# First pair's operand remainders on VectorE, and the down projection's first buffers placed slot by slot and loaded from a new point

## The reference, cut to what matters

```python
def _conv_ffn(h, conv_prev, w_up, conv_w, conv_b, w_down):
    u = h @ w_up                                   # 1024 -> 2 * 2816
    L = u.shape[1]
    ext = jnp.concatenate([conv_prev.astype(u.dtype), u], axis=1)
    c = conv_b + sum(conv_w[j] * ext[:, j:j + L] for j in range(FFN_CONV))
    gate, val = jnp.split(c, 2, axis=-1)
    return (jax.nn.silu(gate) * val) @ w_down, ext[:, -(FFN_CONV - 1):]
```

## Time and profile before

| what | value |
|---|---|
| median of 3 runs | 3153.21 us (3151.97 to 3154.39) |
| profiled execution, its own time | 3155.45 us |
| its span, first to last instruction | 3153.7 us |
| TensorE busy (matmuls) | 3041.2 us, 96% |
| VectorE busy | 1603.9 us, 51% |
| ScalarE busy | 1232.1 us, 39% |
| GpSimd busy | 1069.9 us, 34% |
| mean granted TensorE clock | 0.990 |

### The profile page before, as it was taken

The page is one execution under the profiler, slowest core; times in us unless marked ns, Lnnn a source line. Parts: engine busy times, 40 slices in busy tenths (PEclk is TensorE's granted clock), DMA queues, the critical chain, the costliest instruction groups (busy, mean ns, idle before and its releaser), DMA issues. The chain is left out here.

```text
span 3153.7 us, 51482 instructions
## 1 busy us (share of the span) xinstructions
PE 3041.2 (96%) x19914; PEld 2812.6 (89%) x19914; DVE 1603.9 (51%) x1828; ACT 1232.1 (39%) x1980; POOL 1069.9 (34%) x543
## 2 busy tenths in 40 slices
PE   7899999999999999999998999999989999998998
PEld 6899999999988888888887879999988999997887
DVE  5554355435515655455552131222048888886665
ACT  5244334433434454444354340212244434343433
POOL 2333233323311211121112221343325555554664
PEclk9999999999999999999999999999999999999999
DMA  6312121212136877886778665432322222226554
GB/s 174 95 42 76 56 61 38 74 56 62 56 87 125 154 134 149 155 141 119 147 136 181 165 195 175 150 104 71 109 76 63 64 77 68 70 63 208 196 202 147
DMA packets 737348, 356.63 MB, mean 113 GB/s; under 512 B 377968, under 2 KB 707472, under 8 KB 737248
## 3 DMA queue, kind: packets, MB, share of 16 engines
q1 hardware_dynamic: 731544, 345.88, 43.7%
q10 hardware_dynamic: 5704, 9.39, 0.8%
HBM read 282.04 MB, written 73.15 MB: 113 GB/s over the span
## 5 line engine op out<-in xcount | busy, mean ns | idle before, releaser
L127 POOL TENSOR_TENSOR weight_lo<-weight_stage,weight_hi 128x1024 fp32r<-128x1024 f32 x136 | 344.2, 2533 | 944.4 <-ACT weight_hi L122 944.4
L174 PE MATMUL group<-h_hi_part,weight_hi 128*128 128x384 f32 x912 | 324.1, 355 | 16.1 <-DVE key_rows L772 5.9
L175 PE MATMUL group<-h_lo_part,weight_hi 128*128 128x384 f32 x912 | 310.1, 340 | 0.0
L176 PE MATMUL group<-h_hi_part,weight_lo 128*128 128x384 f32 x912 | 310.0, 340 | 0.0
L122 ACT ACTIVATE weight_hi<-weight_stage 128x1024 fp32r<-128x1024 f32 x136 | 143.9, 1058 | 411.3 <-PE group L3157 241.1
L3155 PE MATMUL group<-h_hi_part,weight_hi 128*128 128x384 f32 (+1 forms) x832 | 270.1, 325 | 2.2 <-PEq L1637 2.2
L3157 PE MATMUL group<-h_hi_part,weight_lo 128*128 128x384 f32 (+1 forms) x832 | 269.6, 324 | 0.0
L3156 PE MATMUL group<-h_lo_part,weight_hi 128*128 128x384 f32 (+1 forms) x832 | 269.4, 324 | 0.0
L1459 PE MATMUL group<-h_hi_part,weight_hi 128*128 128x384 f32 x768 | 268.1, 349 | 1.2 <-ACT next_v L1205 1.0
L1459 PE MATMUL group<-h_hi_part,weight_lo 128*128 128x384 f32 x768 | 261.3, 340 | 0.0
L1459 PE MATMUL group<-h_lo_part,weight_hi 128*128 128x384 f32 x768 | 259.1, 337 | 0.0
(11 more groups left out here) (384 smaller groups left out, 7917.9 us busy)
## 6 DMA issues: line engine op xcount, KB each, us to landing
weight_stage<-in_w_in SPq DMA_DIRECT2D x88, 512.0 KB, 4.8
down_w<-in_w_down SPq DMA_DIRECT2D x66, 512.0 KB, 3.5
cached_v<-in_cache_diff_v SPq DMA_DIRECT2D x128, 256.0 KB, 5.1
cached_k<-in_cache_diff_k SPq DMA_DIRECT2D x224, 128.0 KB, 4.2
gate_in<-scratch_gates SPq DMA_DIRECT2D x24, 576.0 KB, 3.8
down_f<-scratch_y_branch SPq DMA_DIRECT2D x66, 192.0 KB, 3.6
weight_stage<-in_w_branch SPq DMA_DIRECT2D x24, 512.0 KB, 3.9
weight_stage<-in_w_up SPq DMA_DIRECT2D x22, 512.0 KB, 4.7
```

The lines of the kernel that those rows point to most:

```text
L127: pool.tensor_tensor(self.wlo[:, n % 2, :], self.wst[:, n % 2, :], self.whi[:, n % 2, :].bitcast(F32), ALU.subtract).then_inc(self.w_lo, 1)
L174: pe.matmul(out, wh[:, k, :], xh[:, k, cols], start=(k == 0), stop=False)
L175: pe.matmul(out, wh[:, k, :], xl[:, k, cols], start=False, stop=False)
L176: last = pe.matmul(out, wl[:, k, :], xh[:, k, cols], start=False, stop=(k == KT - 1))
```

## The change

- The remainders of the first pair's operands P2, P1, P5 and P6 are made by VectorE, between its quadrant work, instead of GpSimd, which waits for all eight remainders before its first turn. ScalarE makes P5's high part ahead of S4's quadrants, and P6's (with `m2`) ahead of tap 0 of pair 0's value half.
- The buffers of the down projection are placed one by one: those of w slot 0 and f slot 0 in the area of A12, slot 1 in that of A11, slot 2 in that of S1, and f slot 3 in the first half of S2's.
- In the last turn SP waits for `prod` at "P2" of the last pair, loads step 0, waits for "P1", loads step 1, waits for "P5", loads step 2, and only then stores pair 20's result.
- ScalarE, VectorE and GpSimd make the parts of step 2 too within the last turn, ahead of pair 21's value taps.

```diff
-    def operand_lo(pool, t, d, op):
+    def operand_lo(eng, t, d, op):
@@ buffers of the down projection
-    dn.a = Bin(part_at[0], 6 * PART)
-    dn.w = dn.a.take("down_w", [P, 3, D])
-    ...
+    dn.w, dn.whi, dn.wlo, dn.f, dn.fhi, dn.flo = ([] for _ in range(6))
+    spill = Bin(part_at[6], PART)
+    for n in range(4):
+        home = Bin(part_at[2 * n], 2 * PART) if n < 3 else spill
+        if n < 3:
+            for list_, what, dt in ((dn.w, "w", F32), (dn.whi, "w_hi_part", F32R), (dn.wlo, "w_lo_part", F32R)):
+                list_.append(home.take(f"down_{what}{n}", [P, D], dt))
+        for list_, what, dt in ((dn.f, "f", F32), (dn.fhi, "f_hi_part", F32R), (dn.flo, "f_lo_part", F32R)):
+            list_.append(home.take(f"down_{what}{n}", [P, RG], dt))
@@ sync, turn
-            store_f(sp, t, -1)
+            if n < FT - 1:
+                store_f(sp, t, -1)
             if n == FT - 1:
-                wait_op(sp, prod, t, 0, "P5")
-                for s in range(3):
+                wait_op(sp, prod, t, 0, "P2")
+                for s, op in enumerate(("P1", "P5")):
                     load_step(sp, s)
+                    wait_op(sp, prod, t, 0, op)
+                load_step(sp, 2)
+                store_f(sp, t, -1)
@@ scalar
         operand_hi(act, t0, 1, "P1")
         quad_hi("S2", lambda j: mv[:, KH + j, 1], S["sum_2"], 0)
         first_out(3)
+        operand_hi(act, t0, 1, "P5")
         quad_hi("S4", lambda j: mv[:, KH + j, 0], S["sum_4"], 0)
         quad_hi("S3", lambda j: mv[:, j, 0], S["sum_3"], 0)
-        operand_hi(act, t0, 1, "P5")
         for sem, v in ready_x:
             act.wait_ge(sem, v)
         pads(t0, 1, 0)
+        m2(t0, 1)
+        operand_hi(act, t0, 1, "P6")
         tap0(t0, 0, 1)
         news(t0, 0, 1)
-        m2(t0, 1)
-        operand_hi(act, t0, 1, "P6")
@@ scalar, vector and gpsimd, last turn (here scalar's)
-                down_hi(act, 0)
-                down_hi(act, 1)
+                for s in range(3):
+                    down_hi(act, s)
@@ vector
+        operand_lo(dve, t0, 0, "P2")
         combine(dve, t0, 1, 1)
+        operand_lo(dve, t0, 1, "P1")
         for j in range(KH):
             dve.wait_ge(S["sum_2"], j + 1)
             ...
             quad_lo("S2", j, mv[:, KH + j, 1], 5 * KH)
+            if j == 1:
+                operand_lo(dve, t0, 1, "P5")
         combine(dve, t0, 1, 2)
         ...
         for j in range(KH):
             quad_lo("S3", j, mv[:, j, 0], 7 * KH)
+        operand_lo(dve, t0, 1, "P6")
@@ gpsimd
-        operand_lo(pool, t0, 0, "P2")
-        operand_lo(pool, t0, 1, "P1")
-        operand_lo(pool, t0, 1, "P5")
-        operand_lo(pool, t0, 1, "P6")
+        pool.wait_ge(lo_r, 8)
```

More of the change, by code:

```diff
@@ L2181, in operand_hi @@
         act.activation(slot(q)[0], blocks(m)[SOURCE[op]], ACT.Copy).then_inc(hi_r, 1)
-    def operand_lo(pool, t, d, op):
+    def operand_lo(eng, t, d, op):
         q = number(t.n0 + d, op)
         m = t.n0 + d + (op == "P2")
-        wait_op(pool, hi_r, t, d, op)
+        wait_op(eng, hi_r, t, d, op)
         hi, lo = slot(q)
-        pool.tensor_tensor(lo, blocks(m)[SOURCE[op]], hi.bitcast(F32), ALU.subtract).then_inc(lo_r, 1)
+        eng.tensor_tensor(lo, blocks(m)[SOURCE[op]], hi.bitcast(F32), ALU.subtract).then_inc(lo_r, 1)
     PLAIN = ("B21", "B11", "B22", "B12")
@@ L2251, in ffn_phase @@
     dn.sq = dn.b.take("x3_square", [P, 2, D])
-    dn.c = Bin(part_at[6], 2 * PART)
+    dn.c = Bin(part_at[7], PART)
     dn.orow = dn.c.take("new_conv_rows", [P, 2, D])
@@ L2272, in load_step @@
             sp.wait_ge(dn.S["down_w_lo"], s - 2)
-        sp.dma_start(dn.w[:, s % 3, :], g.x["w_down"][0][k * P:(k + 1) * P, :]).then_inc(dn.w_in[s % 3], 16)
+        sp.dma_start(dn.w[s % 3][:], g.x["w_down"][0][k * P:(k + 1) * P, :]).then_inc(dn.w_in[s % 3], 16)
         if s >= 4:
@@ L2278, in load_step @@
         f = g.s["y_branch"].rearrange("n k p r -> (n k) p r")[k][:, gi * RG:(gi + 1) * RG]
-        sp.dma_start(dn.f[:, s % 4, :], f).then_inc(dn.f_in[s % 4], 16)
+        sp.dma_start(dn.f[s % 4][:], f).then_inc(dn.f_in[s % 4], 16)
     def load_x2(sp, gi):
@@ L2333, in down_hi @@
             act.wait_ge(dn.S["down_step"], s - 2)
-        act.activation(dn.whi[:, s % 3, :], dn.w[:, s % 3, :], ACT.Copy).then_inc(dn.S["down_w_hi"], 1)
+        act.activation(dn.whi[s % 3][:], dn.w[s % 3][:], ACT.Copy).then_inc(dn.S["down_w_hi"], 1)
         act.wait_ge(dn.f_in[s % 4], 16 * (s // 4 + 1))
-        act.activation(dn.fhi[:, s % 4, :], dn.f[:, s % 4, :], ACT.Copy).then_inc(dn.S["down_f_hi"], 1)
+        act.activation(dn.fhi[s % 4][:], dn.f[s % 4][:], ACT.Copy).then_inc(dn.S["down_f_hi"], 1)
     def spare_out(act, u):
@@ L2495, in scalar @@
         news(t, -1, 0)
-        down_hi(act, 2)
         silu(t, -1)
@@ L2594, in down_f_lo @@
         dve.wait_ge(dn.S["down_f_hi"], s + 1)
-        dve.tensor_tensor(dn.flo[:, s % 4, :], dn.f[:, s % 4, :], dn.fhi[:, s % 4, :].bitcast(F32), ALU.subtract)\
+        dve.tensor_tensor(dn.flo[s % 4][:], dn.f[s % 4][:], dn.fhi[s % 4][:].bitcast(F32), ALU.subtract)\
             .then_inc(dn.S["down_f_lo"], 1)
@@ L2674, in turn @@
             if n == FT - 1:
-                down_f_lo(dve, 0)
-                down_f_lo(dve, 1)
+                for s in range(3):
+                    down_f_lo(dve, s)
             else:
@@ L2683, in vector @@
         taps(dve, t, -1, 0)
-        down_f_lo(dve, 2)
         product(dve, t, -1)
@@ L2708, in down_w_lo @@
             pool.wait_ge(dn.S["down_w_hi"], s + 1)
-            pool.tensor_tensor(dn.wlo[:, s % 3, :], dn.w[:, s % 3, :], dn.whi[:, s % 3, :].bitcast(F32),
+            pool.tensor_tensor(dn.wlo[s % 3][:], dn.w[s % 3][:], dn.whi[s % 3][:].bitcast(F32),
                                ALU.subtract).then_inc(dn.S["down_w_lo"], 1)
@@ L2732, in turn @@
             else:
-                down_w_lo(0)
-                down_w_lo(1)
+                for s in range(3):
+                    down_w_lo(s)
         turns(pool, turn)
-        down_w_lo(2)
         for s in range(3, STEPS):
@@ L2858, in tensor @@
                 acc = bank[TILE_SLOTS[gi][m]]
-                fh, fl = (f[:, s % 4, m * P:(m + 1) * P] for f in (dn.fhi, dn.flo))
+                fh, fl = (f[s % 4][:, m * P:(m + 1) * P] for f in (dn.fhi, dn.flo))
                 for h in range(2):
                     cols = slice(h * 512, (h + 1) * 512)
-                    wh, wl = dn.whi[:, s % 3, cols], dn.wlo[:, s % 3, cols]
+                    wh, wl = dn.whi[s % 3][:, cols], dn.wlo[s % 3][:, cols]
                     pe.matmul(acc[:, h, :], fh, wh, start=(k == 0), stop=False)
```

## The result

The changed kernel takes 3160.68 us (median of 22 runs), the kernel before 3155.9 us (22 runs beside them): the ratio is 1.0016, with a 95% interval of 1.0010 to 1.0022. It is slower, by 4.8 us between the medians, and by less than the 0.2% that the forecast called a change. One run of the changed kernel took 5946.39 us; it counts in its median and not in the ratio, and no trace shows what happened in it.

The account below looks back on a forecast made before the run. TensorE is busy nearly all the span, but VectorE with ScalarE was taken to set the pace of turns 3 to 17. Terms -1.2 + 3.8 + 1.9 = +4.5 us gave a median of 3157.7 us, range 3152.5 to 3161.5.

Parts of the forecast that it names:

- rival (b): Seam: one burst of loads, store, x2 columns and final row lands parts late; +7.5 us, 3160.7; chance 0.14.
- The first pair: First pair: VectorE, relieved of contention with GpSimd, reaches c11 earlier; 1.2 us gained for the whole kernel.
- TensorE in the first pair: P5 without a wait, 4.0 us before P6 in place of 7.4, then 1.9 us for u4 in turn 1.
- The wait on a product that the pair doesn't have: Seam: SP's wait for P2 means 151 products, so loads start after the last product, 3.85 us later.
- The first landing: Seam: first load lands half of 0.9 us sooner (4.4 now, median 3.5); parts of step 0 3.4 us later.
- The chain to step 3: Seam: late parts 3.4, f remainder ahead of value taps +2.4, freed gate taps -2.0; step 3 +3.8 us.
- The clock at step 3: Down projection: after a 6.6 us wait before step 3 TensorE runs at low clock, adding 1.9 us.
- its lower bound for the chain: Seam: the least delay of step 3, 2.6 + 0.5 = +3.1 us.
- (c): Seam: loads come within the pair; -3.1 us there, -4.3 with the first pair, 3148.9; chance 0.07.
- (d): First pair: VectorE freed longer or TensorE's gain passes in full; -3.9 instead of -1.2, total +1.8, 3155.0; chance 0.09.

Follow-up runs that it names:

- store_first: The changed kernel with pair 20's store issued before SP's waits, as in the kernel before, the three loads still behind the last product; ratio to the kernel before 1.0021.
- step2_late: `loads_early` with step 2's parts back where the kernel before makes them; ratio to the kernel before 0.9974.
- best: `loads_early` with the parts of steps 3 and 4 made before pair 21's Silu and product, and gate taps ahead of c11; 3136.69 us, ratio 0.9943.
- pair_and_taps: The kernel before with the first pair's part of the change and VectorE's gate taps moved ahead of c11, seam as before; ratio 0.9967.
- loads_early: The changed kernel with SP's first wait naming P2 of the pair before, so loads issue within the last pair; 3151.2 us, ratio 0.9984.
- seam_only: The kernel before with only the seam's part of the change (buffer slots, load order and wait, step 2's parts); ratio 1.0017.
- first_only: The kernel before with only the first pair's part of the change (four remainders on VectorE, ScalarE's order, GpSimd's wait); ratio 0.9998.
- best_p6: `best` with P6's high part and remainder made ahead of S3's quadrants; ratio to the kernel before 0.9941.

## Why the prediction was right, and where its terms were off

The forecast was +4.5 us and the median 3157.7 us; measured were +4.8 us and 3160.68 us, and the kernel before itself ran 2.7 us slower here than in the three runs that the forecast started from. That shift, not the change, brought the median to 0.8 us from the end of the range and onto rival (b)'s 3160.7; what bears on the mechanism is the difference. From the stage's start to tile 0 the traces give +3.68 us.

**The first pair, -1.2 us forecast, -1.88 measured.** The mechanism held: VectorE's queue decides, u4 of turn 1 moved by 1.88 us, and so did the last product. Two terms were too pessimistic. VectorE reached the value taps 0.23 us later (2378.99 and 2375.66, each from its stage's start), not 0.5, as four remainders cost 4 x 0.61 = 2.4 us, not 2.6. And it took 4.94 us from the taps to c11 (2378.99 to 2383.93), not 5.3, since only one operation stood beside GpSimd.

**TensorE in the first pair.** P5 without a wait: right. The wait before P6 was 2.33 us, not 4.0, because P2 of pair 1 and the start of P1 ran at the lower of the clock's two levels after a wait of 1.81 us and so ended later; the granted clock there was 0.51 (window 2366 to 2369 us, same columns as above):

```profile
2366.00:2369.00 3.00, 3.00 (x15) 3.00 (x15) 3.00 (x5) 1.70 (x3) 0.00 (x0) 0.51 0.00 0
```

Where that clock stayed at 1.00 (`store_first`, `step2_late`, `best`, `pair_and_taps`), the wait before P6 was 3.8 us, nearly the 4.0. It didn't matter for the sum: TensorE then waited 1.76 us for u4 (1.9 forecast).

**The wait on a product that the pair doesn't have.** Right: the loads start behind the last product, 3.85 us later by its clock (495.59 - 493.62 + 1.88). `loads_early` shows that this alone is the loss.

**The first landing, 4.4 and 3.5 us averaged.** It took 3.2 us, step 0's parts came 2.64 us later instead of 3.4, and step 0 waited 7.24 us, not 8.0. The measured landing agrees with the estimate of 3.2 us that the forecast worked out from the Trainium skill ("DMA: Bandwidth & Descriptors", Anatomy of one DMA) and set aside for the row. The total did not fall with it, because step 0 is not on the chain to step 3. The second weight is: issued 0.87 us later, it took 6.0 us (5.6 before), and that was left out of the sum. ScalarE stood 2.21 us for it, step 1's parts came 3.57 us later, and the f remainders of steps 1 and 2 ended at 2863.06, which is 6.25 us later against the last product than the f remainder of step 1 before, where 5.8 were forecast.

**The chain to step 3, +3.8 forecast, +4.22 measured** (524.67 - 522.33 + 1.88). One more f remainder ahead of the value taps, GpSimd silent beside the gate taps (4.89 to 2.91 us, the 2.0 us of the forecast), the rest of the chain unchanged. Of the 0.4 us, 0.2 are the second landing (3.57 for 3.4) and 0.3 the f remainders (two took 5.10 us where one took 2.42: 2.7 for 2.4).

**The clock at step 3, +1.9 forecast, +1.34 measured** (tile 0's shift of 3.68 less step 3's of 2.34), behind a wait of 7.40 us (6.6). In `seam_only` and `store_first` the same step lost 2.2 and 2.7 us.

**The sum.** -1.88 + 4.22 + 1.34 = 3.68 against -1.2 + 3.8 + 1.9 = 4.5: the errors of three terms partly cancelled. Two slips of the forecast's arithmetic changed nothing: its lower bound for the chain takes 2.6 us for the delay of the parts, below its own 3.0 (2.64 was measured for step 0), and 0.10 and 0.10 make 0.20, not 0.19, on the slow side. The runs' 4.8 us (ratio 1.0010 to 1.0022, so 3.2 to 6.9 us) hold both.

**The rivals.** (c), loads within the pair, was put at -4.3 against before; as `loads_early` it is -4.2 by tile 0 and ratio 0.9984. That the sums agree is partly luck: -1.9 for the first pair (-1.2 forecast) and -2.3 for the seam (-3.1). (d) is excluded by `first_only`, (b) by the landings and by `store_first`; the x2 columns and the final row were not moved.

## What to carry to other kernels

Before giving a saved wait on the busiest engine its full price, look for the small wait that it shows in every turn of the loop behind: 0.2 us a turn said here that VectorE set the pace, and exchanging two lines there won 7 us by the trace, more than the whole change with its wait put right (4.2 in `loads_early`). A wait that names a step by a computed number deserves a look at the first and last turn, where the step may not exist; one index decided here between +4.8 and -5 us. And a part that is made earlier only helps if the next thing after it isn't held by the same queue. In the traces, short waits gathered into one also cost more than apart, through the clock (`loads_early` against `step2_late`, `best_p6` against `best`); the timed runs do not separate these pairs.

## What the runs showed of the hardware that was not expected

- The start of the stage lay between 2346.0 and 2359.9 us in the profiled executions of kernels whose code up to there is the same. Single executions can't be compared by their spans at this size of effect; distances within a stage mostly agreed to 0.1 us (u4 of turn 1: 37.68 to 37.70 us in six kernels).
- But not always. In turn 1 of `seam_only`, with the code of the kernel before, VectorE's combination began 42.36 us from the stage's start and GpSimd's remainder 0.02 us after it: 0.68 us for VectorE, 1.82 for GpSimd. In the kernel before GpSimd began first, by 0.11 us: 1.78 for VectorE, 1.34 for GpSimd. Of these 1.1 us 1.04 were left at the last product.
- The lower clock after a wait is not a fixed price. After 7.40, 7.48 and 6.33 us step 3 lost 1.3, 2.7 and 2.2 us; after 1.81 us in the first pair it came as well (granted clock 0.51), while the kernel before kept full clock after 2.33 us at the same place, and so did `store_first`, `step2_late`, `best` and `pair_and_taps` after 1.8 us with the same code there. A difference of 1 to 2 us between two traces can be this alone.
- Of two 512 KB loads issued 0.87 us apart, with a load of 192 KB between them and nothing else under way, the first landed after 3.2 us and the second after 6.0 us. In `loads_early`, where they lie over 3 us apart, each takes 3.3 to 3.4 us.
